# mLSTM phase: gate rows spread over the partitions by DMA instead of by TensorE, and more projection pieces in the first round of a head

## The reference

```
b = cumsum(logf);  log_d[t,s] = b[t] - b[s] + i[s]  (s <= t);  m_t = max(b_t + m_prev, max_s log_d[t,s])
num = exp(b + m - m_t) * (q C) + (q k^T * exp(log_d - m_t)) v
qn  = exp(b + m - m_t) * (q n) + sum_s(q k^T * exp(log_d - m_t))
h   = num / max(|qn|, exp(-m_t))
C, n, m = decayed by exp(b_last + m - m_new), plus the chunk's weighted k v^T, k, and the new maximum
```

## Time and profile before

| what | value |
| --- | --- |
| median of 3 executions | 3392.69 us (3390.32 to 3394.24) |
| the profiled execution | 3392.9 us, of which 3391.2 us are the span from the first to the last instruction |
| TensorE busy | 3115.3 us, 92% of the span |
| mean granted TensorE clock | 0.965 |
| the loop over the mLSTM heads | from 2009 to 2443 us of the span |

### The profile page before, as it was taken

One profiled execution on the slowest core, in us unless ns is written; L12 is line 12 of the kernel. 1 busy time (PEld: TensorE's weight loads), 2 busy tenths in 40 slices (PEclk: granted clock), 3 DMA queues, 4 the chain that ended last, 5 costly groups with the idle time before them and its releaser, 6 DMA issues. The chain is left out here.

```text
span 3391.2 us, 54197 instructions
## 1 busy us (share of the span) xinstructions
PE 3115.3 (92%) x19666; PEld 2993.4 (88%) x19666; DVE 1526.8 (45%) x3265; ACT 838.0 (25%) x1761; POOL 1152.3 (34%) x991
## 2 busy tenths in 40 slices
PE   5988998899876999999999799999679999999998
PEld 5888888888766999999999689999679999999997
DVE  4567666666643433333433433433334333334334
ACT  2333343334422210011101224444312101110112
POOL 3333232323115443444343141312055334443430
PEclk8999999999978999999999899999789999999999
DMA  3000100010003111111111110101031111111101
GB/s 130 26 22 13 27 21 21 12 27 21 2 3 114 50 44 43 45 48 49 43 37 37 51 45 21 39 21 32 2 114 51 50 37 53 45 43 43 49 25 51
DMA packets 206909, 136.67 MB, mean 40 GB/s; under 512 B 32120, under 2 KB 198832, under 8 KB 206576
## 3 DMA queue, kind: packets, MB, share of 16 engines
q1 hardware_dynamic: 206832, 135.63, 13.5%
HBM read 120.98 MB, written 14.63 MB: 40 GB/s over the span
## 5 line engine op out<-in xcount | busy, mean ns | idle before, releaser
L91 PE MATMUL ps<-act_hi,ffn_hi 128*128 128x352 f32 x2496 | 811.7, 325 | 61.4 <-POOL ffn_lo L147 59.9
L93 PE MATMUL ps<-act_hi,ffn_lo 128*128 128x352 f32 x2496 | 804.8, 322 | 0.0
L92 PE MATMUL ps<-act_lo,ffn_hi 128*128 128x352 f32 x2496 | 804.0, 322 | 0.0
L145 POOL TENSOR_TENSOR ffn_hi<-ffn_stage,one 128x512 fp32r<-128x512 f32 x296 | 320.4, 1082 | 1033.9 <-PE ps L93 899.0
L91 PEld LDWEIGHTS ps<-act_hi,ffn_hi 128*128 128x128 f32 x2496 | 471.0, 189 | 67.0 <-issue 53.8
L92 PEld LDWEIGHTS ps<-act_lo,ffn_hi 128*128 128x128 f32 x2496 | 472.2, 189 | 0.8 <-issue 0.2
L93 PEld LDWEIGHTS ps<-act_hi,ffn_lo 128*128 128x128 f32 x2496 | 471.3, 189 | 0.0
L147 POOL TENSOR_TENSOR ffn_lo<-ffn_stage,ffn_hi 128x512 fp32r<-128x512 f32 x296 | 407.0, 1375 | 23.2
L750 DVE TENSOR_TENSOR x<-x,ps 128x352 f32<-128x352 f32 x528 | 273.2, 521 | 212.9 <-PE ps L93 212.9
L92 PE MATMUL ps<-ffn_hid_lo,ffn_hi 128*128 128x352 f32 x1056 | 341.4, 323 | 0.0
L93 PE MATMUL ps<-ffn_hid_hi,ffn_lo 128*128 128x352 f32 x1056 | 340.8, 323 | 0.0
(11 more groups left out here) (314 smaller groups left out, 5161.4 us busy)
## 6 DMA issues: line engine op xcount, KB each, us to landing
ffn_stage<-in_ffn_w_gu SPq DMA_DIRECT2D x88, 512.0 KB, 3.7
ffn_stage<-in_ffn_w_down SPq DMA_DIRECT2D x44, 512.0 KB, 3.5
gdn_stage<-in_gdn_w_in SPq DMA_DIRECT2D x32, 512.0 KB, 4.1
x_kept<-x SPq DMA_DIRECT2D x2, 4224.0 KB, 12.8
x<-x_kept SPq DMA_DIRECT2D x6, 1408.0 KB, 7.8
ml_stage<-in_ml_w_in SPq DMA_DIRECT2D x16, 512.0 KB, 4.2
load_rows<-in_x_prompt SPq DMA_DIRECT2D x8, 512.0 KB, 4.4
ffn_stage<-in_gdn_w_out SPq DMA_DIRECT2D x8, 512.0 KB, 4.0
```

The source lines that it names most:

```text
L91: pe.matmul(out, w_hi, rhs_hi, start=first, stop=False)
L92: pe.matmul(out, w_hi, rhs_lo, start=False, stop=False)
L93: return pe.matmul(out, w_lo, rhs_hi, start=False, stop=last)
L145: nc.gpsimd.tensor_tensor(hi, st, one, ALU.mult).then_inc(self.hi_done, 1)
```

## The change

The two gate quantities are turned into rows once, at the end of the prologue: TensorE transposes all 72 columns of each (steps 56 to 57), VectorE copies them out (steps 58 and 59), and SyncE stores them in a DRAM tensor `ml_gate_rows`. From there ScalarE's queue loads three rows of 128 values at a time, spread over all 128 partitions: `peaks` into `pe_exp`, `floors` into `floor`, which has three buffers now. The peak rows of the next round are requested at the end of a round's `prepare`, once pt has been made from the same buffer; the floor rows of the next head are requested at three places of the head before it. `rows_of` goes from TensorE, with its six calls in a head (18 products of two passes each), and the transposed values no longer wait for q_scale and the exponents. ScalarE issues six DMAs in a head. `FILL` goes from (3, 4, 4, 4) to (6, 3, 3, 3): the first round of a head gets three more pieces and each of the others one fewer.

```diff
@@ -1669,7 +1669,7 @@
     ps = tk.ps
     B = 3
     U = B * NU
-    FILL = (3, 4, 4, 4)
+    FILL = (6, 3, 3, 3)
     W_QK = HEADS * MDK
     w_in = a["ml_w_in"][0].rearrange("(k p) f -> p k f", p=P)
     NQ = 5
@@ -1690,7 +1690,7 @@
         rs = buf("rs", [P, NU, UNIT], F32)
         pe_exp = buf("exponents", [P, BATCHES, P], F32)
         q_scale = buf("q_scale", [P, BATCHES, P], F32)
-        floor = buf("floor", [P, 2, BATCHES, P], F32)
+        floor = buf("floor", [P, BATCHES, BATCHES, P], F32)
         pt = buf("pt", [P, 2, BATCHES, P], F32)
         qs = buf("qs", [P, 2, BATCHES, P], F32)
         kw = buf("kw", [P, 2, BATCHES, P], F32)
@@ -1709,6 +1709,7 @@
                 start = 2 * W_QK + (b - 1) * D + ahead * P
                 ws.load(sp, t * B + (ahead * B + b), b, w_in[:, :, bass.ds(t * P + start, P)])
 
+        rows_dram = nc.dram_tensor("ml_gate_rows", (TILES, HEADS, 2, P), F32).ap()
         full_rows = (qkv[MDK:P, 0:2, 0:TOK], qs[MDK:P], kw[:, :, :, MDK:P], state[MDK:P])
         pro = mlstm_prologue(nc, tk, sem, buf, a, w_in, ws, gates, gain, m_end, qkv, v_tok, num[0:2 * HEADS], full_rows)
         unit_done, evacuated = sem("unit_done"), sem("evacuated")
@@ -1721,6 +1722,7 @@
                                                       sem("rs_done"))
         negative_done, den2_done, clamped = sem("negative_done"), sem("den2_done"), sem("clamped")
         o_normed, final_done, m_out = sem("o_normed"), sem("final_done"), sem("m_stored")
+        rows_stored, peak_in, floor_in = sem("rows_stored"), sem("peak_landed"), [sem(f"floor_landed{r}") for r in range(BATCHES)]
         block = ctx.enter_context(nc.Block())
 
         @block.sync
@@ -1758,6 +1760,8 @@
             weights(0, 0, 2)
             states(0)
             weights(0, 1, 0)
+            sp.wait_ge(pro.step, 59)
+            sp.dma_start(rows_dram.rearrange("c h q p -> (c h) q p"), pro.rows[:]).then_inc(rows_stored, 16)
             with sp.Fori(0, HEADS - 2) as t:
                 head(t, 2)
             head(HEADS - 2, 1)
@@ -1809,18 +1813,9 @@
                 if third == 2:
                     mm.then_inc(unit_done, 1)
 
-            def rows_of(bank, q, r):
-
-                for i in range(BATCHES):
-                    c = 3 * r + i
-                    mm = pe.matmul(ps[:, bank, i * P:(i + 1) * P], hg[:, q, c:c + 1].to_broadcast([P, P]),
-                                   tk.ident[:], start=True, stop=True)
-                mm.then_inc(prep_done, 1)
-
             def prepare(t, r, pieces):
                 if r > 0:
                     pe.wait_ge(tok_done, t * 6 + 2 * r)
-                rows_of(2, 1, r)
                 if r > 0:
                     pe.wait_ge(made, t * 6 + 2 * r)
                 for i in range(BATCHES):
@@ -1828,16 +1823,11 @@
                     mm = pe.matmul(ps[:, 3, i * P:(i + 1) * P], qkv[:, 1, cols], qkv[:, 0, cols],
                                    start=True, stop=True)
                 mm.then_inc(prep_done, 1)
-                if r > 0:
-                    pe.wait_ge(floor_done, t * 3 + r)
-                rows_of(4, 2, r)
                 for i in range(BATCHES):
                     mm = pe.transpose(ps[:, 5, i * P:(i + 1) * P], qkv[:, 1, (3 * r + i) * P:(3 * r + i + 1) * P],
                                       tk.ident[:])
                 mm.then_inc(prep_done, 1)
                 pieces(2)
-                pe.wait_ge(qsc_done, t * 3 + (r + 1))
-                pe.wait_ge(e_done, t * 3 + (r + 1))
                 for i in range(BATCHES):
                     mm = pe.transpose(ps[:, 2, i * P:(i + 1) * P], qkv[:, 2, (3 * r + i) * P:(3 * r + i + 1) * P], tk.ident[:])
                 mm.then_inc(prep_done, 1)
@@ -1930,32 +1920,49 @@
                 place = tk.x[:, bass.ds(t, 1), unit_cols(n)].rearrange("p a t -> p (a t)")
                 nc.scalar.activation(place, place, ACT.Sigmoid).then_inc(gated, 1)
 
-            def prepare(t, r, pieces):
+            def rows_of(h, q, r):
+
+                return rows_dram[3 * r:3 * r + 3, bass.ds(h, 1), q].rearrange("c a p -> a c p").to_broadcast([P, BATCHES, P])
+
+            def peaks(h, r):
+                act.sem_inc(ws.act_checked, 1)
+                nc.scalar.dma_start(pe_exp[:], rows_of(h, 0, r)).then_inc(peak_in, 16)
+
+            def floors(h, r):
+                act.sem_inc(ws.act_checked, 1)
+                nc.scalar.dma_start(floor[:, r], rows_of(h, 1, r)).then_inc(floor_in[r], 16)
+
+            def prepare(t, r, pieces, more):
                 par = r % 2
                 grid = lambda bank: ps[:, bank, 0:3 * P].rearrange("p (i c) -> p i c", i=3)
-                act.wait_ge(prep_done, t * 15 + (5 * r + 1))
+                act.wait_ge(peak_in, t * 48 + (16 * r + 16))
                 if r > 0:
                     act.wait_ge(made, t * 6 + 2 * r)
                 for i in range(BATCHES):
                     c = 3 * r + i
-                    op = nc.scalar.activation(q_scale[:, i], ps[:, 2, i * P:(i + 1) * P], ACT.Exp,
+                    op = nc.scalar.activation(q_scale[:, i], pe_exp[:, i], ACT.Exp,
                                               bias=hg[:, 4, c:c + 1], scale=-1.0)
                 op.then_inc(qsc_done, 1)
                 act.wait_ge(e_done, t * 3 + (r + 1))
                 nc.scalar.activation(pe_exp[:], pe_exp[:], ACT.Exp, scale=-1.0).then_inc(exp_done, 1)
-                act.wait_ge(prep_done, t * 15 + (5 * r + 3))
+                act.wait_ge(floor_in[r], t * 16 + 16)
                 if r == 2:
-                    act.wait_ge(den_done, t * 9 + 3)
                     act.wait_ge(chain, t * 18 + 6)
-                nc.scalar.activation(floor[:, par], grid(4), ACT.Exp, scale=-1.0).then_inc(floor_done, 1)
-                act.wait_ge(prep_done, t * 15 + (5 * r + 4))
+                nc.scalar.activation(floor[:, r], floor[:, r], ACT.Exp, scale=-1.0).then_inc(floor_done, 1)
+                act.wait_ge(prep_done, t * 9 + (3 * r + 2))
                 for i in range(BATCHES):
                     c = 3 * r + i
                     op = nc.scalar.mul(kw[:, par, i, 0:MDK], ps[:, 5, i * P:i * P + MDK], hg[:, 3, c:c + 1])
                 op.then_inc(tok_done, 1)
                 pieces(2)
-                act.wait_ge(prep_done, t * 15 + (5 * r + 5))
+                act.wait_ge(prep_done, t * 9 + (3 * r + 3))
                 nc.scalar.copy(v_tok[:, par, :, 0:DV], grid(2)).then_inc(tok_done, 1)
+                if r < 2 or more:
+                    act.wait_ge(made, t * 6 + (2 * r + 1))
+                    peaks(t, r + 1) if r < 2 else peaks(t + 1, 0)
+                if r == 2 and more:
+                    act.wait_ge(den_done, t * 9 + 3)
+                    floors(t + 1, 0)
 
             def chunk(t, r, i):
                 c = 3 * r + i
@@ -1975,11 +1982,14 @@
                 act.wait_ge(cols_done, t + 1)
                 for r in range(BATCHES + 1):
                     if r < BATCHES:
-                        prepare(t, r, pieces)
+                        prepare(t, r, pieces, more)
                     for i in range(BATCHES):
                         pieces(FILL[r] // BATCHES + (i < FILL[r] % BATCHES))
                         if r > 0:
                             chunk(t, r - 1, i)
+                        if (r, i) == (3, 0) and more:
+                            act.wait_ge(den_done, t * 9 + 6)
+                            floors(t + 1, 1)
                         if (r, i) == (2, 0):
 
                             for u in range(NU):
@@ -1987,6 +1997,8 @@
                             nc.scalar.preload_act_table_set("natural_log_exp_and_others")
                 act.wait_ge(num_done, t * 9 + 9)
                 act.wait_ge(den_done, t * 9 + 9)
+                if more:
+                    floors(t + 1, 2)
 
                 nc.scalar.activation(den[:, 0:TOK], den[:, 0:TOK], ACT.Square,
                                      scale=math.sqrt(DV * RMS_EPS)).then_inc(den2_done, 1)
@@ -2006,6 +2018,10 @@
                 if u == 3:
                     pro.scalar_last(act)
                 evacuate(0, u, True)
+            act.wait_ge(rows_stored, 16)
+            peaks(0, 0)
+            for r in range(BATCHES):
+                floors(0, r)
             with act.Fori(0, HEADS - 1) as t:
                 head(t, True)
             head(HEADS - 1, False)
@@ -2018,16 +2034,15 @@
 
             def prepare(t, r):
                 par = r % 2
-                dve.wait_ge(prep_done, t * 15 + (5 * r + 1))
                 dve.wait_ge(qsc_done, t * 3 + (r + 1))
                 for i in range(BATCHES):
                     c = 3 * r + i
-                    op = nc.vector.scalar_tensor_tensor(out=pe_exp[:, i], in0=ps[:, 2, i * P:(i + 1) * P],
+                    op = nc.vector.scalar_tensor_tensor(out=pe_exp[:, i], in0=pe_exp[:, i],
                                                         scalar=hg[:, 0, c:c + 1], in1=tk.later_neg[:],
```

(18 more changed lines are left out.)

## The result

The changed kernel takes 3415.52 us (median of 5 executions, 3406.18 to 3421.94) against 3393.53 us for the kernel before beside it (3390.32 to 3398.41). The ratio is 1.0062, with a 95% interval of 1.0042 to 1.0082: slower by 22 us. The profiled execution is the slowest of the five, 3421.94 us, which is 29.0 more than the 3392.9 of before.

A forecast was written before the change was run, and what follows sets the result against it. TensorE's work was taken to bound seven heads, with the weight chain nearly as long in six. Head 0 -3.0, six heads +2.8, clock +10.2, last head +1.2: +11.2 on 3392.9 gives 3404.1 us, range 3386 to 3420.

The forecast's parts named there:

- Landing: a broadcast load took 2.5 us: ScalarE's row loads: 2.5 us from issue to landing, taken from a profile row of a broadcast load.
- hidden: Peak rows of round 1: land at about T+19 (T: a head's stores start), needed by TensorE only at chunk 0.
- contention term: Row loads sharing DMA engines with weight loads delay block 1 by 0 to 0.54 us; 0.3 taken in each of six heads.
- the last head: Head without projection pieces: -0.5 us for row groups gone against late peak rows, +1.7 for the clock; together +1.2.
- The rival of a dear issue: ScalarE's DMA issue takes 1.1 us instead of 0.52, delaying copies and sigmoids; 3414 us, chance 0.12.
- The weight chain: Stores confirmed, weights loaded, block 1 split: piece 9 cannot start before T+26.15 in six heads; TensorE waits about 3.4 us.
- T to the end of the split: Sign: from the start of a head's stores (T) to GpSimd finishing block 1's split stays at 26 to 27 us.
- The removed work: TensorE in a head: six row-matmul groups gone, 4.0 us, and the value transposes' wait gone, 0.77 us.
- Head 0: First head of the loop, its blocks loaded long before, keeps the gains: -4.0 + 0.2 + 0.8 = -3.0 us.
- FILL: New piece table puts six-matmul pieces between chunks 0 and 1 and 4 and 5; loses 0.8 us in each of seven heads.
- The clock: TensorE's clock falls behind each wait of 3 to 3.4 us: 1.7 us in each of six heads, 10.2 us.
- The rival of the work gained: Weights are in time and removed work is gained: -27.5 us, 3365; chance 0.13 for gain in whole or good part.

The follow-up runs named there:

- a_distinct: The changed kernel with each partition's row loads reading its own places in DRAM, gate rows' values left out; 3392.81 us, 1.0002 to the kernel before.
- a_early: The changed kernel with SyncE loading weight blocks 1 and 2 before a head's stores instead of behind them; 3419.31 us, 1.0075 to the kernel before.
- a_distinct_gated: The changed kernel with row loads from different DRAM places, weight blocks requested a head ahead, GpSimd's splits placed in VectorE's gaps; 3373.50 us, 0.9942 to the kernel before.
- a_distinct_early: The changed kernel with row loads from different DRAM places and weight blocks 1 and 2 loaded before the stores; 3395.16 us, 1.0014 to the kernel before.

## Why the prediction held, and where it did not

The sign and the range held: 3404.1 was forecast, 3386 to 3420, and 3415.5 came. The size forecast was half of the measured one: +11.2 against +22.0. That the time still lay in the range is in part luck, since two errors of the sum went against each other.

*The step that failed* is "Landing: a broadcast load took 2.5 us", with the conclusion "hidden". The row had a load of 4 KB that I took for one of 192 KB from 384 packets. It measured 6.5 to 7.0, which brought three things: the load of block 1 slowed by about 4 us in three of six heads, in place of the contention term's 0.3 in each; ScalarE's waits reached TensorE; and the last head, for which I took +1.2, lost 5.4. The rival of a dear issue did not come, since an issue takes 0.38 to 0.50 us.

*The weight chain* was right as a mechanism. a_distinct, in which the landing is what I assumed, shows the wait for L147 in each of the six heads after the first, 3.04 us in the mean where I had 3.4. In the changed kernel TensorE waits for L147 in all six as well, but that the sum of 22.8 us is near 3.4 x 6 = 20.4 is chance: the waits are 0.60 to 7.43. My sign that T to the end of the split stays at 26 to 27 us failed there: it was 23.2 to 30.0. Why the stores are confirmed earlier than before stays open. It was also the decisive wait only in part: a_early shows that taking it away gives nothing while GpSimd's split then falls on VectorE.

*The removed work.* Forecast: 4.0 of row matmuls and 0.77 of wait, less 0.8 of FILL, 4.0 a head. a_distinct_gated has four heads that are 3.5 us shorter. Head 0 was forecast at -3.0; in a_distinct it takes 44.0 us instead of 47.1. With the slow loads it was +3.3.

*FILL* at 0.8 a head measured 0.86 in the kernel before, half of it a wait that the forecast did not have.

*The clock* at 1.7 in each of six heads, 10.2: in a_distinct four stretches of 3.4 us, 6.8 us of price. In the changed kernel the stretches in the six heads are 6.8, 3.4, 3.4, 10.2 and 6.8 long; what is left of the six heads' +20.7 after -21.0 of work and +30.7 of waits (22.8 and 7.9) is 11.0. The stretches add up to 30.6 us; 9.4 of them lie inside TensorE's stalls, where a low clock costs nothing, and half of the rest is 10.6, near the 11.0.

*An error that another hid.* With the landing that I assumed, the kernel is a_distinct, and it takes 3392.8, not 3404.1. Six heads there are 4.7 us longer than before, forecast 13.0 (fewer and shorter stalls, two heads without a fall of the clock), and the last head is 1.8 shorter, forecast +1.2. So my sum was some 11 us too high for its own premises, and the landing that I assumed made it 22.7 too low.

*The rival of the work gained* (3365) "decides if block 1 is split by T+22.8". That is necessary and not enough: a_distinct_early has it split in time and stands at 3395.2; with the split placed as well it is 3373.5.

## What to carry to other kernels

Work taken from the bounding engine is gained only when the next wait has gone too, so after each fix look at which wait came in its place: here the weight chain hid GpSimd's collision with VectorE, and both hid ScalarE's wait for its rows. A transfer made early also makes early what it triggers; place the work that it triggers on one engine (here GpSimd) in a gap of the engine that it disturbs (here VectorE). When one small piece of DRAM is to be spread over all partitions, measure that load itself: lay it out as one long run, make a few copies early enough that the first reader does not wait for them, and do not take the landing of a tiny load for it.

## What the runs showed of the hardware

A load of 192 KB in which 128 partitions read the same three rows of DRAM in 384 packets of 512 B lands after 6.0 to 7.0 us (medians); with the same packets from different places for each partition after 2.6; from one place in 128 packets of 1536 B after 3.1. The slow one also slows a 512 KB load beside it on another queue, from 4.3 to 8.4 us in the stretch shown. It did so to the first of two such loads only where it was issued before them or at most 0.28 us behind their start (three heads), not where it came 0.69 us or more behind (three heads).

The Trainium skill ("DMA: Bandwidth & Descriptors", section "Issuing engines are not separate DMA queues") has DMAs of all issuing engines share the same 16 engines. That the weight load slowed by 4 us agrees with it, but by the packets' count alone the term would have been 0.54; that the packets themselves get slower (48 ns instead of 30) is what the runs add.

VectorE operations on two SBUF inputs of 128x352 take 1.06 to 1.60 us beside a GpSimd operation instead of 0.53 to 0.58.
